# Where weights and activations of a two block transformer stand in SBUF, modulo 512 bytes

## What is computed

```
def swiglu(x, w1, w3, w2):
    return (jax.nn.silu(x @ w1) * (x @ w3)) @ w2

def _merge(h, outs, gates, w_br, w_merge, b_merge, w_out):
    yb = jnp.stack([o * jax.nn.silu(z) for o, z in zip(outs, gates)], axis=2)
    y = jnp.einsum('bnrw,rwd->bnrd', yb, w_br)
    g = jax.nn.sigmoid(h @ w_merge + b_merge).reshape(b, n, N_BRANCH, D_MODEL)
    return jnp.sum(g * y, axis=2) @ w_out
...
def reference(x, ...):
    x = first_block(x, ...)     # hybrid_ab, FFN, nsa, FFN, norm
    return second_block(x, ...) # two layers of _layer, each ending in _merge
```

## The kernel before, in words

| weights less activations, modulo 512 bytes | before | after |
|---|---|---|
| XX, high weights on XH / high on XL | 0 / 0 | 320 / 64 |
| XX, low weights on XH | 0 | 320 |
| XX in the second block's first layer (512 columns) | 0 | 0 |
| hidden | 288 | 320 (64 for its low part) |
| merged, branches_low1, first layer (512 columns) | 288 | 0 |
| branches, branches_low0, first layer (512 columns) | 160 | 0 |
| merged, second layer (256 columns), high part / low part | 288 / 288 | 320 / 64 |
| branches, second layer (256 columns), high part / low part | 160 / 160 or 288 | 320 / 64 |
| turned products (activations less streaming weights) | 0 | 192 / 448, or 0 in the first layer |
| early, high part of tile k / low part | 160 - 8k / 96 - 8k | the same |

## Time and profile before

### The profile page before, as it was taken

The page is one execution under the profiler, slowest core; times in us unless marked ns, Lnnn a source line. Parts: engine busy times, 40 slices in busy tenths (PEclk is TensorE's granted clock), DMA queues, the critical chain, the costliest instruction groups (busy, mean ns, idle before and its releaser), DMA issues.

```text
span 1382.0 us, 22584 instructions
## 1 busy us (share of the span) xinstructions
PE 1365.3 (99%) x9250; PEld 1170.3 (85%) x9250; DVE 846.8 (61%) x1299; ACT 661.8 (48%) x1170; POOL 147.4 (11%) x131
## 2 busy tenths in 40 slices
PE   8999999999999999999999999999999999999999
PEld 8988888889955888888887877888888888879999
DVE  6976887656867678885734467433333456775554
ACT  6646555544366465555433446332233346555442
POOL 0010111001310001110004000111011100301110
PEclk9999999999999999999999999999999999999999
DMA  8535667556497455555433210232222234414553
GB/s 306 192 122 183 214 218 251 196 187 200 161 345 263 163 183 192 188 187 182 153 103 103 84 62 32 76 105 94 92 92 92 92 113 140 155 58 153 192 184 123
DMA packets 60967, 215.29 MB, mean 156 GB/s; under 512 B 6721, under 2 KB 12737, under 8 KB 57409
## 3 DMA queue, kind: packets, MB, share of 16 engines
q1 hardware_dynamic: 56272, 206.59, 44.7%
q10 hardware_dynamic: 4592, 7.26, 1.4%
HBM read 208.59 MB, written 1.05 MB: 152 GB/s over the span
## 4 chain that ended last, share of the span: by engine, by line
PE 91%; DVE 4%; ACT 2%; DMA 1%; issue 1%; POOL 0%; SPq 0%; DVEq 0%; ACTq 0%; POOLq 0%
PE psum L330 18%; PE psum L320 16%; PE psum L321 16%; PE psum L322 16%; PE psum L329 8%; PE psum L1275 3%; PE psum L1300 2%; PE psum L317 2%; PE psum L318 2%; PE psum L319 2%; PE psum L1438 2%; DVE WL L252 1%; PE psum L2740 1%; DMA stage<-ab_in 1%; PE psum L1631 1%; PE psum L332 1%
## 5 line engine op out<-in xcount | busy, mean ns | idle before, releaser
L252 DVE TENSOR_TENSOR WL<-stage,WH 128x1024 fp32r<-128x1024 f32 x332 | 419.0, 1303 | 236.0 <-ACT WH L247 235.8
L247 ACT ACTIVATE WH<-stage 128x1024 fp32r<-128x1024 f32 x332 | 333.0, 1051 | 206.7 <-PE psum L322 150.3
L320 PE MATMUL psum<-XX,WH 128*128 128x256 f32 (+1 forms) x1208 | 391.5, 324 | 6.1 <-DVE WL L756 1.7
L321 PE MATMUL psum<-XX,WH 128*128 128x256 f32 (+1 forms) x1208 | 384.5, 318 | 0.0
L322 PE MATMUL psum<-XX,WL 128*128 128x256 f32 (+1 forms) x1208 | 384.2, 318 | 0.0
L330 PE MATMUL psum<-XX,WH 128*128 128x512 f32 x832 | 288.2, 397 | 0.0
L320 PEld LDWEIGHTS psum<-XX,WH 128*128 128x128 f32 x1208 | 229.0, 190 | 36.5 <-issue 9.4
L322 PEld LDWEIGHTS psum<-XX,WL 128*128 128x128 f32 x1208 | 229.1, 190 | 16.1
L321 PEld LDWEIGHTS psum<-XX,WH 128*128 128x128 f32 x1208 | 229.2, 190 | 16.1 <-issue 0.5
L329 PE MATMUL psum<-XX,WL 128*128 128x256 f32 x728 | 203.2, 279 | 0.9 <-DVE WL L252 0.9
L330 PEld LDWEIGHTS psum<-XX,WH 128*128 128x128 f32 x832 | 150.1, 188 | 29.5 <-issue 1.2
(11 more groups left out here) (298 smaller groups left out, 1900.6 us busy)
## 6 DMA issues: line engine op xcount, KB each, us to landing
stage<-w SPq DMA_DIRECT2D x132, 512.0 KB, 4.6
stage<-merge SPq DMA_DIRECT2D x80, 512.0 KB, 4.6
ring<-ada SPq DMA_DIRECT2D x24, 1024.0 KB, 6.0
stage<-in SPq DMA_DIRECT2D x44, 512.0 KB, 4.6
stage<-ab_in SPq DMA_DIRECT2D x22, 512.0 KB, 5.9
stage<-nsa_in SPq DMA_DIRECT2D x20, 512.0 KB, 4.8
stage<-out SPq DMA_DIRECT2D x16, 512.0 KB, 4.8
stage<-ab_out SPq DMA_DIRECT2D x8, 512.0 KB, 4.4
```

The lines of the kernel that those rows point to most:

```text
L247: e.activation(hi, raw, ACT.Copy).then_inc(s_hi, 1)
L252: e.tensor_tensor(lo, raw, hi.bitcast(F32), ALU.subtract).then_inc(s_lo, 1)
L320: e.matmul(dst, wh, xh, start=start, stop=False)
L321: e.matmul(dst, wh, xl, start=False, stop=False)
```

## The change

Unused columns are put ahead of ring, X and arena (40, 88 and 72 of them), and a smaller scratch for DMA descriptors makes room. High parts start 48 columns (192 bytes) and low parts 112 columns (448 bytes) behind a multiple of 512 bytes from the weights, in the first block and in the second block's second layer; in the second block's first layer they start at that multiple itself (XX0, `x, hi, lo`). All 22 inner tiles of the FFN lie in hidden, and F.sg has moved up behind it. The functions of the second block get their activations as L.x; those lines are left out here but for one of them.

```
-ARENA = 14510
+ARENA = 18608
+HI, LO = 48, 112
...
+        sb("before_ring", 40)
         with nc.sbuf_tensor("branches", [128, 4096], F32R) as zh, nc.sbuf_tensor("branches_low0", [128, 2048], F32R) as zl0:
...
+        sb("before_x", 88)
         X = sb("X", 4096)[:, :].rearrange("p (k n) -> p k n", k=8)
-        XX = sb("XX", 8192, F32R)[:, :].rearrange("p (s k n) -> p s k n", s=2, k=8)
+        def shifted(v, n):
+            return v[:, HI:HI + 2 * (n + LO - HI)].rearrange("p (s q) -> p s q", s=2)[:, :, 0:n]
+
+        both = sb("XX", 8448, F32R)
+        XX0 = both[:, 0:8192].rearrange("p (s k n) -> p s k n", s=2, k=8)
+        XX = shifted(both, 4096).rearrange("p s (k n) -> p s k n", k=8)
         XH, XL = XX[:, 0], XX[:, 1]
...
-        with nc.sbuf_tensor("arena_below", [128, 5632], F32), nc.sbuf_tensor("hidden", [128, 7168], F32R) as hid:
-            HH = hid[:, :].rearrange("p (s a n) -> p s a n", s=2, a=14)
+        sb("before_arena", 72)
+        with nc.sbuf_tensor("arena_below", [128, 5632], F32), nc.sbuf_tensor("hidden", [128, 11440], F32R) as hid:
+            HH = shifted(hid, 5632).rearrange("p s (a n) -> p s a n", a=22)
...
-        F.sg = [view(12800 + 512 * n, 512, **two) for n in range(3)]
+        F.sg = [view(17072 + 512 * n, 512, **two) for n in range(3)]
 
         def hidden(k):
 
-            return XX[:, :, k, NOW] if k < 8 else HH[:, :, k - 8, :]
+            return HH[:, :, k, :]
...
-                self.MH, self.ML = [v[:, 0:8 * NT].rearrange("p (k n) -> p k n", k=8) for v in (mh, ml)]
+                x, hi, lo = (XX0, 0, 0) if l == 0 else (XX, HI, LO)
+                self.x = x[:, 0], x[:, 1]
+                self.MH, self.ML = [v[:, at:at + 8 * NT].rearrange("p (k n) -> p k n", k=8) for v, at in ((mh, hi), (ml, lo))]
...
-                z = [v[:, 0:w * NT].rearrange("p (r a n) -> p r a n", r=w // 2, a=2) for v, w in ((zh, 8), (zl0, 4), (zl1, 4))]
+                z = [v[:, at:at + w * NT].rearrange("p (r a n) -> p r a n", r=w // 2, a=2)
+                     for v, w, at in ((zh, 8, hi), (zl0, 4, lo), (zl1, 4, lo))]
...
-                features(e, b[:, 0:NT], w, a * 128, f"l{l}.o{r}{a}", x, L.xs())
+                features(e, b[:, 0:NT], w, a * 128, f"l{l}.o{r}{a}", x, L.xs(), L.x)
...
-    nc = _bacc.Bacc("TRN2", target_bir_lowering=False, num_devices=1)
+    nc = _bacc.Bacc("TRN2", target_bir_lowering=False, num_devices=1, dynamic_dma_scratch_size=2048)
```

More of the change, by code:

```diff
@@ L348, in features, with rows @@
             last.then_inc(*pe.tick(name))
-        def rows(e, dst, w, t, cols, name, x=None, base=0):
+        def rows(e, dst, w, t, cols, name, x=None, base=0, parts=(XH, XL)):
             xs = slice(base + t * 128, base + t * 128 + 128)
@@ L355, in rows @@
                     x(k)
-                last = product(e, dst, w, k, cols, XH[:, k, xs], XL[:, k, xs], k == 0, k == 7, turned=True)
+                last = product(e, dst, w, k, cols, parts[0][:, k, xs], parts[1][:, k, xs], k == 0, k == 7, turned=True)
             last.then_inc(*pe.tick(name))
@@ L461, in adapted_scalar @@
         def adapted_scalar(e, p, shift, t, xs):
+            x = (XX0, XX)[p[1] == "1"]
             for k in range(8):
                 e.wait_ge(*ve.of(f"{p}.t{k}"))
-                e.activation(XH[:, k, xs], t[:, k, :], ACT.Identity, bias=shift(k)).then_inc(*ac.tick(f"{p}.xh{k}"))
+                e.activation(x[:, 0, k, xs], t[:, k, :], ACT.Identity, bias=shift(k)).then_inc(*ac.tick(f"{p}.xh{k}"))
                 yield
@@ L2166, in all_keys_tensor @@
                 x = (lambda k: e.wait_ge(*ve.of(f"n{l}1.x{k}"))) if br == 0 else None
-                features(e, b, w, br * 128, f"k{l}{br}.k", x, slice(0, 512))
+                features(e, b, w, br * 128, f"k{l}{br}.k", x, slice(0, 512), L.x)
             w.done()
@@ L2174, in all_keys_tensor @@
                         sums_tensor(e, L, t)
-                    rows(e, b[:, t * 256:(t + 1) * 256], w, 2 * j + t, slice(0, 256), f"l{l}.v{j}")
+                    rows(e, b[:, t * 256:(t + 1) * 256], w, 2 * j + t, slice(0, 256), f"l{l}.v{j}", parts=L.x)
                 if j == 1:
@@ L2193, in context_keys_tensor @@
             for br in range(2):
-                features(e, keys[br][:, CTX], wk, br * 128, f"k{l}{br}.ck", lambda k: between(br, k), CTX)
+                features(e, keys[br][:, CTX], wk, br * 128, f"k{l}{br}.ck", lambda k: between(br, k), CTX, L.x)
             def values(j):
@@ L2198, in values @@
                 for t in range(2):
-                    rows(e, b[:, t * 256:(t + 1) * 256], wv, 2 * j + t, slice(0, 256), f"l{l}.v{j}")
+                    rows(e, b[:, t * 256:(t + 1) * 256], wv, 2 * j + t, slice(0, 256), f"l{l}.v{j}", parts=L.x)
             values(1)
@@ L2204, in context_keys_tensor @@
                 for br in range(2):
-                    t = product(e, keys[br][:, NOW], wk, k, slice(br * 128, br * 128 + 128), XH[:, k, NOW], XL[:, k, NOW],
+                    t = product(e, keys[br][:, NOW], wk, k, slice(br * 128, br * 128 + 128), L.x[0][:, k, NOW], L.x[1][:, k, NOW],
                                 k == 0, k == 7)
@@ L2409, in rest_tensor @@
                 for t in range(2):
-                    rows(e, b[:, t * 256:(t + 1) * 256], w, 2 * j + t, slice(0, 256), f"l{l}.vt{j}")
+                    rows(e, b[:, t * 256:(t + 1) * 256], w, 2 * j + t, slice(0, 256), f"l{l}.vt{j}", parts=L.x)
                     if br is not None and j + t == 0:
@@ L2457, in product_of @@
                 b = tile(e, f"l{l}.{name}{a}", 1, s)
-                features(e, b[:, 0:NT], w[c], a * 128, f"l{l}.{name}{a}", None, L.xs())
+                features(e, b[:, 0:NT], w[c], a * 128, f"l{l}.{name}{a}", None, L.xs(), L.x)
                 if a == 1:
@@ L2516, in gate @@
                 for k in ks:
-                    t = product(e, b[:, 0:NT], w["merge"], 8 * m + k, slice(0, 128), XH[:, k, 0:NT], XL[:, k, 0:NT], k == 0,
+                    t = product(e, b[:, 0:NT], w["merge"], 8 * m + k, slice(0, 128), L.x[0][:, k, 0:NT], L.x[1][:, k, 0:NT], k == 0,
                                 k == 7)
```

7 lines of the change are left out of this document (4 added, 3 removed).

## The result

The changed kernel takes **1375.65 us** (median of 6 runs, 1374.83 to 1376.96), the kernel before beside it 1386.32 (6 runs, 1382.7 to 1388.54). The ratio is 0.9929, with a 95% interval of 0.9916 to 0.9943: 10.7 us faster, 0.7%. The forecast was 1369.3, its range 1346 to 1385. The profiled execution spans 1373.3 us where that of before spans 1382.0.

The account below looks back on a forecast made before the run. TensorE, busy for 1365.3 of 1382.0 us, was taken as the bound, as one stream of products costing their spacing of starts. Terms of -2.9, -10.4, -1.1 and -4.1 sum to -18.5 us, giving 1369.3 us, range 1346 to 1385.

Parts of the forecast that it names:

- Term 1: 512 column products of branches and merged go from distance 160 or 288 to 0: -2.9 us, the surest term.
- Term 2: 2304 plain 256 column products on XX go from 120 to 115.5 ns: -10.4 us, ends -3.9 and -25.
- term 3: 384 products of 256 columns on branches and merged go from 118.3 to 115.5 ns: -1.1 us.
- Terms 6 and 7: L1300's 128 column products at new distances, and the FFN's first eight inner tiles moved to hidden: 0 us each.
- The rival of no gain for 256 columns: 256 column products gain nothing and the 512 column gain stays: 1385 us, to 1388 if pairs lose it; chance 0.15.
- the floor of 109 ns: Load and stream never meet: 109 ns for 256 columns, 340 for a pair, -41 us, 1347 us; chance 0.12.
- term 4: FFN pairs of a 512 and a 256 column product, on XX and hidden, go to 345 ns: -4.1 us.
- The argument against: A pair at distance 0 doesn't reach 226.7 for its 512 columns either, since 355 leaves 235 beside 120.
- Term 5: Products with activations as weights (L317 to L319): 336 get distances 192 and 448, taken as 0, between -2.4 and +1.7 us.
- Term 8: Weight supply keeps up: 220 GB/s with DMA engines 0.65 busy becomes 223, so any cost is hidden.
- the sentence that all of the sum lies on the path: All -18.5 us shorten the kernel's time, as TensorE waits for next to nothing; the span goes from 1382.0 to 1363.5.

Follow-up runs that it names:

- experiment 12: Changed kernel with every distance 0 and the FFN's first eight inner tiles back in XX: 1381.57 us, ratio 0.9981 to the kernel before.
- experiment 1: Changed kernel with every distance back at 0, new layout and inner tiles' place kept: 1382.79 us, ratio 0.9974 to the kernel before.
- experiment 5: Microbenchmark of TensorE alone, distance by distance: plain 256 column products 113.3 or 117.8 ns at 320 / 64, 120.0 at 0; pairs 346.7 to 353.3 ns.
- experiment 8: Microbenchmark of TensorE alone with the kernel's tile strides, other engines idle, then at work: pairs at 64 took 353.3 ns and at 96 346.7 in both halves.
- experiment 7: Changed kernel with the FFN's pairs written as three products of 256 columns: 1365.64 us, ratio 0.987 to the kernel before.
- experiment 3: Changed kernel with high parts at 64 and low parts at 320, inner tiles at 256 and 384: 1380.21 us, ratio 0.9964 to the kernel before.
- experiment 4: Changed kernel with high and low parts both at 64, inner tiles at 448 and at 0 / 256: 1377.69 us, ratio 0.9942 to the kernel before.
- experiment 6: Changed kernel measured again with nothing edited: 1376.95 us, ratio 0.9952 to the kernel before.
- experiment 9: Changed kernel with high and low parts both at 96, inner tiles at 160 and 224: 1378.09 us, ratio 0.9953 to the kernel before.
- experiment 2: Changed kernel with high and low parts both at 320, inner tiles at 128 and 192: 1378.36 us, ratio 0.9954 to the kernel before.
- experiment 10: Changed kernel with every distance 0 and the FFN's pairs as three products of 256 columns: 1390.23 us, ratio 1.0037 to the kernel before.
- experiment 11: The kernel with high and low parts both at 64 measured again, nothing edited: 1376.41 us, ratio 0.9939 to the kernel before.

## Why the prediction came out as it did

**Right by its steps.** Term 1 (512 columns to distance 0): -2.7 for -2.9. Term 2 (256 columns on XX): -10.1 for -10.4, though not as it was reasoned. I took one spacing of 115.5 between bounds; it is a mixture of 113.3 and 117.8, and that its mean came so near is luck: some 720 of these products stand in the last layer, and had that layer taken 117.8, as in the five profiles of other kernels at 64 and 320, term 2 would be 3.2 us smaller and term 3 1.7. Term 3: -2.0 for -1.1, since branches and merged fell wholly into the cheaper stretch. Terms 6 and 7, nothing: the earlier trace rows stayed, and experiment 12 shows it for the tiles. The rival of no gain for 256 columns is out by experiment 1, and the floor of 109 ns was seen in no steady stretch of 256 column products of any run.

**The step that failed is term 4, the pairs:** +1.9 us for -4.1. I took a pair as a 512 and a 256 column product that would each take its own best, 345 of a possible 340. The 512 column product leaves its best place: 47 plain ones on XX went from 228 to 235, and in the pairs of experiment 5 it takes 235.0 at 64. The 256 column product beside it takes 118.3 there and not 113.3, in all of the segments at 64. So a pair costs 353.3 at 64; 346.7 is the best of any place. And at 0 it was not always dear: in experiments 5 and 8 it takes 346.7 or 353 at 0, and in the kernel before some four in ten of its pairs on XX stood at 347, which the changed kernel's never do. The argument against, which I had written down myself (355 leaves 235 beside 120), was the better one. What would have won is giving pairs up, which the forecast didn't weigh: experiment 7.

**Term 5**, turned products: -1.1 for 0, inside its bounds.

**Term 8, that what supplies TensorE keeps up, and the sentence that all of the sum lies on the path, were too simple.** The kinds above other than "everything else" and waits give -14.5; 5.8 of it came back. The page has 3.4 us more idle time. One place can be read in full, around 380 us, where L1450 waits for the ring. The timelines, first of the changed kernel, then of the one before:

```profile
378.28 1.07 PE L1450 MATMUL psum<-ring,con 128*32 128x256 f32 x16
...
382.48 1.49 PE L1450 MATMUL psum<-ring,con 128*32 128x256 f32 x16 [2.15 <-DMA ring<-ada]
...
386.27 1.94 PE L1450 MATMUL psum<-ring,con 128*32 128x256 f32 x16
```
```profile
380.29 1.07 PE L1438 MATMUL psum<-ring,con 128*32 128x256 f32 x16
...
383.63 1.07 PE L1438 MATMUL psum<-ring,con 128*32 128x256 f32 x16 [1.30 <-DMA ring<-ada]
...
386.34 1.07 PE L1438 MATMUL psum<-ring,con 128*32 128x256 f32 x16
```

TensorE came 2.0 us earlier (378.28 for 380.29), and the transfer was ready only 1.15 us earlier, so 0.85 stayed in the wait. After it the groups of 16 took 1.49 and 1.94 us where they had taken 1.07, as the granted clock of that window was 0.66 and not 1.00: part of it at the 1.2 GHz level, behind the wait. By the third row the lead is 0.07. Together, from 372 to 391 us, some 2.7 us are lost.

The twelve profiles of the whole kernel agree on when the clock falls there. Where the wait for the ring at this place was 1.9 us or longer (1.9 in experiment 3, 2.15 above, 2.3 in 4, 2.5 in 6, 3.0 in 9), the window from 380 to 390 us has a clock of 0.66 to 0.70; where it was 0.5 to 1.5 us (experiments 1, 2, 7, 10, 11, 12 and the kernel before), it has 1.00. In the changed kernel TensorE came earlier and waited longer, so the change may well bring the lower clock on more often; experiment 7, earlier still, waited only 0.5 us and kept its clock, and no run sets the wait alone. Nor does the lower clock need the change: the kernel before has executions with a mean clock of 0.999 or 1.000, most at 1382.6 to 1384.0 us, and others at 0.996 to 0.998 (1384.8 to 1388.4), and its profile was one at full clock. In the changed kernel the clock doesn't explain the spread: its two executions at 1.000 took 1376.74 and 1376.96 us, the longest of the six. They may have taken the dearer spacing in the last layer; they have no trace.

The rest of what came back, some 3.1 us, is spread: in the first 125 us, where weights and inputs arrive, five waits became 0.3 to 0.5 us longer and one 1.2 us, while two shrank by 0.8 and 0.5. The products among the first 1000 matmuls saved 2.9 us, and TensorE was 1.5 us ahead behind them. Four later waits grew by 0.3 to 0.4 us, at 352, 482, 1182 and 1198 us. I didn't test that part by itself.

Against the forecast, the 9.8 us missing from the span are 6.0 of pairs and 5.8 of supply, less some 2 by which terms 3, 5 and the 512 column products on XX did better.

**The median came out nearer than the span, by luck.** The span fell by 8.7 us where 18.5 were forecast, less than half; the median missed by only 6.4. The forecast laid on 5.8 us because the median of the runs before lay so far above the span. Of these, 1.8 are the time outside the span, which every execution shows; the other 4.0 come from setting a median of three, two of them at 1387.8 and 1388.5, against a profile at full clock. For the changed kernel the same distance is 2.3 us (1375.65 less 1373.3), so 3.5 of the 9.8 us don't show in the median.

## What to carry to other kernels

Where a kernel is one stream of float32r products, read the spacing of starts by operand, not the busy time, and set it beside where the weights stand modulo 256 bytes from what streams: here 64 was best for 256 columns, and 0 for 512 among the four places seen (0, 32, 64 and 160). Choose form and place together: three products of 256 columns beat a 512 and a 256 by 12 ns at 64, and lost by 7 to 10 us in all at 0. And expect a shorter TensorE time to come back in part as longer waits wherever the supply was only just in time.

## What the runs showed of the hardware

- The spacing of products depends on the address of the weights in load less that of the streaming operand, with a period of 256 bytes: 120.0 ns at 0 and 256, 118.3 at 32 and 288, 113.3 or 117.8 at 64 and 320, for 256 columns. The Trainium skill, page "TensorE: Matmul & The Clock Gate", section "Step-by-step: what each phase is for", says that the two operands are read through independent ports and a load takes nothing from the running product. By that rule the place would be worth nothing, and the runs don't agree: with everything back at 0 the ratio was 0.9974, beside 0.9929 and 0.9952 for the change, 3 to 6 us, and every long stretch of plain products was back at 120.0 ns. What inside the engine makes the difference no run shows.
- At 64 and 320 a stream takes one of two spacings at its start and keeps it until it is interrupted, over 932 products in the last layer and over 1535 in the FFN of experiment 7. The microbenchmark with the kernel's strides drew the dearer one in 13 of 96 segments, with or without traffic of other engines. In the kernel it is more common: some one in three of the changed kernel's long stretches have it, and in the last layer it held in five of the seven profiles of kernels at 64 and 320, all but the two of the changed kernel. What draws it stays open: traffic didn't change how often it came, and equal segments differ only in when they begin.
- A 512 and a 256 column product in turn, each with its load, cost 353.3 ns at 64, 346.7 at 96 and 224, 351.1 at 128, and one of two values at 0 (346.7 or 353). Neither the tiles' strides nor 97% busy VectorE and ScalarE changed it by more than 0.5 ns at any of these places.
- The granted clock fell to 0.66 to 0.70 in the window from 380 to 390 us in the five profiles in which TensorE had waited there for 1.9 to 3.0 us, and stayed at 1.00 in the seven with a wait of 0.5 to 1.5 us. That the wait's length is the cause isn't shown, since no run changed it alone.
